# Two layers on one core: activation table sets loaded by name, a pair's output kept one step later, and the last four head pairs in a new order with rotary products on 32-row quarters

## The chip, the cores and the metric

One Trainium2 chip, one of its cores. The metric is the device time of one execution in microseconds (us), lower is better. Engine names: PE is TensorE, DVE is VectorE, ACT is ScalarE, POOL is GpSimd, SP is SyncE. The kernel is one hand-scheduled program: each engine runs its own list of instructions in order, and the lists meet only at semaphores.

## The reference, cut to what matters

512 tokens of width 1024 go through two different layers. The first is a feed-forward half, an attention part and another feed-forward half; the second is a modulated layer with a convolution, a chunked recurrence (rwkv) and a feed-forward part with a short convolution. The change touches the attention of the first layer and the activation functions of ACT.

```python
def chunked_relbias_attention(q, k, v, rel_bias):      # heads "A": 8 heads of 64, bias from a table
    ...
        sc = jnp.einsum('bihd,bjhd->bhij', q_blk, kb).astype(jnp.float32) * scale
        sc = sc + bias[None]
...
def mla_attention(c_q, c_kv, k_rope, ...):             # heads "B": 8 heads of 64 + 32
    q_nope = rmsnorm(q[..., :B_NOPE], q_nope_norm)
    q_pe = apply_rope(rmsnorm(q[..., B_NOPE:], q_rope_norm), cos, sin)
    k_nope = rmsnorm(kv[..., :B_NOPE], k_nope_norm)
    k_pe = apply_rope(rmsnorm(k_rope, k_rope_norm)[:, :, None, :], cos, sin)
    q_full = jnp.concatenate([q_nope, q_pe], axis=-1)
    k_full = jnp.concatenate([k_nope, jnp.broadcast_to(k_pe, (b, s, B_HEADS, B_ROPE))], axis=-1)
    return block_causal_attention(q_full, k_full, v)
```

So a score of a B head is a product over 64 "nope" rows plus a product over 32 rotary rows, and the rotary key is the same for all eight heads. In the second layer `sigmoid`, `tanh`, `exp`, `log`-based inverse roots and `silu` follow each other on ACT.

## The kernel before, in words

Activations lie with features on the 128 partitions and 512 tokens along the free axis. Weights come in 264 slabs of 128 x 1024 through a ring of four (`RING`); SP loads a slab, POOL splits it in a high and a low part (`split`, L607 and L609), and PE multiplies in three passes (`product`, L735 to L737).

**Attention.** Heads go in pairs `p` = 0 to 7 (0 to 3 are A heads, 4 to 7 are B heads), each with four blocks of 128 queries `qb` = 0 to 3 and `L` = 128 (qb + 1) keys. A step `t` is one pair and one block, in the order p, qb: 32 steps. PE runs a loop over `i`; in one turn of it stand, in this order, `scores(i + 1)`, `turn(i - 2)` (the transposes of the probabilities, L1032) and `values(i - 3)` (probabilities times values, L1048). Scores of A heads use 64 rows of the array for each of the two heads (L1018); those of B heads need 96 rows, so one head of a pair after the other (L1021), and SP first copies rows together for them (`rows_moved`, 24 transfers of its queue, L558 to L564). Beside PE:

- DVE at step `i`: `score_max(i)` (add bias or mask, row minimum, two instructions, L2185), `keep_turned(i - 3)` (PSUM to SBUF for the second head, L2200), `row_recip(i - 1)` (L2192), and where a pair ends `out_lo(p)` (L2205).
- ACT at step `i`: `keep_turned(i - 3)` for the first head (L1694), `softmax(i)` (two Exp, L1684), and where a pair ends `out_hi(p)` (L1699).
- POOL: `probs_scaled(t)` (L625), and in three of four steps of pairs 1 to 3 a part of the rotary embedding (L635 to L640).

The scores of a step lie in two of the banks 0 to 3, so `scores(t)` waits until DVE has read step t - 2 (`row_nmax`, 2 (t - 1)). The output of a pair lies in bank 6 + p % 2; the first `values` of pair p therefore waits for `out_lo(p - 2)`:

```python
if qb == 0 and p >= 2:
    pe.wait_ge(S("o_made"), p - 1)
```

`out_hi(p)` and `out_lo(p)` stand at `i == last_step(p) + 4`. At the end of the loop three products of the next stage (`out1_begun`) are put between the last steps of attention.

**Activation functions.** ACT holds one set of function tables at a time. Where a function is needed that is not surely loaded, the compiler puts a load before it (ACT_TABLE_LOAD in the trace). In the second layer `inverse_root` (L1758 Ln, L1761 Exp) runs in `key_rs` and `centred_rs`; `recurrence(half)` calls `key_rs(1)` in half 0 and `centred_rs(0)` in half 1, between moves of PSUM results (`move`, L1751) that PE waits for. `centred(1)` moves and squares the last results (L1751, L1853), and PE sums the squares (L1297) before it begins the product `out2`.

## Time and profile before

| | us |
|---|---|
| median of 3 runs | 1695.97 (1695.22 to 1697.27) |
| profiled execution, its own time | 1695.5 |
| span in the profile | 1693.7 |
| PE busy | 1652.9 |
| POOL, DVE, ACT busy | 998.2, 946.2, 429.6 |
| mean granted TensorE clock | 0.992 |

The profile shows one execution. The span runs from the first to the last recorded instruction; the execution's own time is 1.8 us longer. In timelines a row gives start, duration, engine, line, operation, output and inputs, shapes and how many records are merged; a matmul of plain float32 leaves two records. A bracket gives the idle time before the row and what ended it.

### The profile page before, as it was taken

Reading aid. Unit: us, or ns where it says so; the run is one execution under the profiler, and the core shown is the slowest. Engines: PE = TensorE matmul, PEld = TensorE weight load, DVE = VectorE, ACT = ScalarE, POOL = GpSimd, SP = SyncE. Lnnn points to the kernel's source line nnn. Section 1 sums busy time; section 2 is a strip of 40 time slices with the busy share of each in tenths; the row PEclk is TensorE's granted clock in tenths of the full one; section 3 lists DMA queues with packets and bytes.
Section 4 is the critical chain, followed back from the end, with each engine's and each line's share of the span. In section 5 each row is a group of like instructions: output and inputs, shape, how many; then the busy total and the mean of one; then the engine's idle time right before and its main releaser. Section 6 shows DMA issues by size and latency. Waiting matters only on the chain.

```text
span 1693.7 us, 26731 instructions
## 1 busy us (share of the span) xinstructions
PE 1652.9 (98%) x10086; PEld 1349.5 (80%) x10086; DVE 946.2 (56%) x1381; ACT 429.6 (25%) x713; POOL 998.2 (59%) x626
## 2 busy tenths in 40 slices
PE   8999999999999999999999999998989999999998
PEld 6888888888766778888888867887868788888887
DVE  5665551226656347555562259987766765665003
ACT  4000000015866321111100031234453333233001
POOL 3666666776565367666677744611205576666674
PEclk9999999999999999999999999999999899999999
DMA  6444443333241134444443322210002232233332
GB/s 211 145 149 148 142 144 124 100 99 125 77 118 45 51 110 144 141 149 149 149 149 104 107 90 73 92 63 3 3 2 91 72 99 94 92 99 99 102 110 87
DMA packets 52400, 175.80 MB, mean 104 GB/s; under 512 B 6369, under 2 KB 8801, under 8 KB 52193
## 3 DMA queue, kind: packets, MB, share of 16 engines
q1 hardware_dynamic: 43056, 144.64, 26.4%
q10 hardware_dynamic: 9264, 30.02, 5.6%
q8 instruction: 60, 0.98, 0.2%
q14 instruction: 20, 0.16, 0.0%
HBM read 169.66 MB, written 2.10 MB: 101 GB/s over the span
## 4 chain that ended last, share of the span: by engine, by line
PE 92%; DVE 3%; ACT 3%; issue 1%; POOL 1%; DMA 0%; ACTq 0%; DVEq 0%; POOLq 0%; SPq 0%
PE banks L735 25%; PE banks L736 25%; PE banks L737 25%; PE banks L1190 4%; PE banks L1021 1%; PE banks L1048 1%; PE banks L767 1%; PE banks L773 1%; PE banks L768 1%; PE banks L1032 1%; PE banks L855 1%; PE banks L1018 1%; PE banks L808 1%; PE banks L1165 1%; PE banks L810 0%
## 5 line engine op out<-in xcount | busy, mean ns | idle before, releaser
L609 POOL TENSOR_TENSOR w_lo<-w_raw,w_hi 128x1024 fp32r<-128x1024 f32 x256 | 635.2, 2481 | 21.4
L607 POOL TENSOR_SCALAR w_hi<-w_raw 128x1024 fp32r<-128x1024 f32 x256 | 288.9, 1129 | 546.5 <-DMA w_raw<-in_slabs 469.3
L735 PE MATMUL banks<-h_hi,w_hi 128*128 128x512 f32 x1376 | 539.8, 392 | 0.6 <-POOL w_lo L609 0.5
L737 PE MATMUL banks<-h_hi,w_lo 128*128 128x512 f32 x1376 | 535.6, 389 | 0.0
L736 PE MATMUL banks<-h_lo,w_hi 128*128 128x512 f32 x1376 | 535.4, 389 | 0.0
L735 PEld LDWEIGHTS banks<-h_hi,w_hi 128*128 128x128 f32 x1376 | 258.3, 188 | 61.4 <-issue 6.8
L736 PEld LDWEIGHTS banks<-h_lo,w_hi 128*128 128x128 f32 x1376 | 258.4, 188 | 54.0 <-issue 1.2
L737 PEld LDWEIGHTS banks<-h_hi,w_lo 128*128 128x128 f32 x1376 | 258.3, 188 | 53.7
L735 PE MATMUL banks<-act_hi,w_hi 128*128 128x512 f32 (+1 forms) x550 | 209.6, 381 | 0.0
L736 PE MATMUL banks<-act_lo,w_hi 128*128 128x512 f32 (+1 forms) x550 | 209.3, 381 | 0.0
L737 PE MATMUL banks<-act_hi,w_lo 128*128 128x512 f32 (+1 forms) x550 | 209.3, 381 | 0.0
L1630 ACT ACTIVATE tmp<-tmp 128x512 f32<-128x512 f32 x44 | 27.9, 634 | 360.9 <-DVE tmp L2033 360.9
L737 PEld LDWEIGHTS banks<-act_hi,w_lo 128*128 128x128 f32 x550 | 103.4, 188 | 19.9
L735 PEld LDWEIGHTS banks<-act_hi,w_hi 128*128 128x128 f32 x550 | 103.4, 188 | 19.9
L736 PEld LDWEIGHTS banks<-act_lo,w_hi 128*128 128x128 f32 x550 | 103.4, 188 | 19.4
L2073 DVE SCALAR_TENSOR_TENSOR xT<-banks,xT 128x512 f32<-128x512 f32 x24 | 16.6, 691 | 168.7 <-PE banks L737 168.7
L2033 DVE TENSOR_TENSOR tmp<-banks,tmp 128x512 f32<-128x512 f32 x44 | 30.5, 692 | 142.0 <-PE banks L737 137.8
L2025 DVE TENSOR_TENSOR act_lo<-tmp,act_hi 128x512 f32 x66 | 105.2, 1594 | 8.1
L2047 DVE CUSTOM_DVE_ANT_0 adaw<-adaw,silc 128x1024 f32<-128x1024 f32 x48 | 76.0, 1583 | 4.9 <-DMA adaw<-in_ada 4.5
L2589 DVE SCALAR_TENSOR_TENSOR tmp<-banks,vec,tmp 128x511 f32<-128x511 f32 x44 | 32.8, 746 | 75.8 <-ACT tmp L1925 75.8
L2038 DVE TENSOR_TENSOR tmp<-tmp 128x512 f32<-128x512 f32 x44 | 63.1, 1435 | 8.6 <-ACT tmp L1630 8.6
L1190 PEld LDWEIGHTS banks<-in_arena 64*64 64x64 f32 x1792 | 59.5, 134 | 10.5 <-issue 6.9
(384 smaller groups left out, 1837.6 us busy)
## 6 DMA issues: line engine op xcount, KB each, us to landing
w_raw<-in_slabs SPq DMA_DIRECT2D x260, 512.0 KB, 3.5
adaw<-in_ada ACTq DMA_DIRECT2D x48, 512.0 KB, 3.6
relb<-in_relb ACTq DMA_DIRECT2D x8, 256.0 KB, 2.9
out_y<-xT SPq DMA_DIRECT2D x16, 128.0 KB, 1.8
w_raw<-in_slabs SPq DMA_DIRECT2D x4, 256.0 KB, 5.3
xT<-in_x SPq DMA_DIRECT2D x1, 1024.0 KB, 8.9
block<-in_block ACTq DMA_DIRECT2D x1, 704.0 KB, 7.1
xT<-in_x SPq DMA_DIRECT2D x2, 256.0 KB, 3.9
```

Source lines behind the costliest of these rows:

```text
L607: nc.gpsimd.tensor_scalar(w_hi[:, r, :], w_raw[:, r, :], 1.0, 1.0, ALU.mult, ALU.mult).then_inc(S("w_hi"), 1)
L609: nc.gpsimd.tensor_tensor(w_lo[:, r, :], w_raw[:, r, :], w_hi[:, r, :], ALU.subtract).then_inc(S("w_split"), 1)
L735: mm(out, hi, rhs_hi, start=start, stop=False, skip_group_check=True)
L736: mm(out, hi, rhs_lo, start=False, stop=False, skip_group_check=True)
L737: return mm(out, lo, rhs_hi, start=False, stop=stop, skip_group_check=True)
L1190: last = mm(out, block_of(lhs, operands, e, g, c), r, start=opens and i == 0, stop=i == len(pairs) - 1, skip_group_check=True)
L1630: f(tmp[:, 2 + u, :], tmp[:, 2 + u, :], ACT.Silu).then_inc(S("silu"), 1)
L2025: v.tensor_tensor(actl_t[:, bass.ds(at * T, T)], t, hi, ALU.subtract).then_inc(S("act_lo"), 1)
L2033: v.tensor_tensor(tmp[:, 2 + u, :], bank[2 * u], tmp[:, 0, :], ALU.mult).then_inc(S("gate_scaled"), 1)
L2038: v.tensor_tensor(tmp[:, 4 + u, :], tmp[:, 2 + u, :], tmp[:, 4 + u, :], ALU.mult)\
L2047: v.tensor_tensor_reduce(out=adaw[:, u, :], in0=adaw[:, u, :], in1=silc, scale=1.0, scalar=0.0, op0=ALU.mult, op1=ALU.add, accum_out=mod_s ...
L2589: v.scalar_tensor_tensor(out=tmp[:, n, 1:T], in0=bank[n][:, 0:T - 1], scalar=w[1], in1=tmp[:, n, 1:T], op0=ALU.mult, op1=ALU.add).then_inc ...
```

## The change

Five places name a table set ahead of its use. Attention of the pairs 4 and 5, then 6 and 7, goes block by block with the two pairs in turn (4, 5, 4, 5, ...), and PE issues the scores of two steps together: four products on 64 rows, then four rotary products on 32 rows each that add to the same banks. The rotary key is copied to all four row quarters (three transfers) and the 24 transfers of `rows_moved` go. Probabilities of these steps use six slots instead of four (four tiles of the bias table are reused). `out_hi` and `out_lo` of pairs 0 to 5 stand at `last_step(p) + 5`. `turn(2)` stands ahead of `scores(5)`, and the third `out1_begun` behind the last `values`.

```diff
         def pair_step(t):
-            p, qb = divmod(t, NT)
+            if t < 4 * NT:
+                p, qb = divmod(t, NT)
+            else:
+                two, r = divmod(t - 4 * NT, 2 * NT)
+                p, qb = 4 + 2 * two + r % 2, r // 2
             return p, qb, P * (qb + 1)
...
         def prob_of(t, e):
-            return prob[:, 2 * (t % 4) + e, 0:pair_step(t)[2]]
+            n = 2 * (t % 4 if t < 4 * NT else (t - 4 * NT) % 6) + e
+            return (prob[:, n, :] if n < 8 else relb[:, n - 8, :])[:, 0:pair_step(t)[2]]
 
         def last_step(p):
-            return NT * p + NT - 1
+            return NT * p + NT - 1 if p < 4 else 4 * NT + 2 * NT * (p // 2 - 1) - 2 + p % 2
+
+        def kept_at(p):
+            return last_step(p) + (5 if p < 6 else 4)
...
-            def rows_moved():
...
+            def key_rows_copied():
+                sp.wait_ge(S("roped"), 3)
+                for a in range(32, P, 32):
+                    sp.dma_start(kr[a:a + 32, 0, :], kr[0:32, 0, :]).then_inc(S("key_rows"), 16)
...
             def scores(t):
...
-                if t >= 4 * NT and qb == 0:
-                    pe.wait_ge(S("rows_moved"), 96 * (p - 3))
                 if t >= 2:
                     pe.wait_ge(S("row_nmax"), 2 * (t - 1))
...
+                q, k = (qa, ka) if p < 4 else (qn, kn)
                 for e in range(2):
-                    mm(out[e][:, 0:L], head_rows(qn, p - 4, e)[:, qs], head_rows(kn, p - 4, e)[:, 0:L], start=True, stop=True)\
-                        .then_inc(S("scores"), 1)
+                    e64 = slice(CH * e, CH * e + CH)
+                    last = mm(score_bank(t, e)[:, 0:L], q[e64, p % 4, qs], k[e64, p % 4, 0:L], start=True, stop=p < 4,
+                              skip_group_check=True)
+                    if p < 4:
+                        last.then_inc(S("scores"), 1)
+
+            def rotary_scores(t):
+                p, qb, L = pair_step(t)
+                if t == 4 * NT:
+                    pe.wait_ge(S("key_rows"), 48)
+                pe.wait_ge(S("roped"), 6 if p < 6 else 9)
+                for i in range(4):
+                    r = slice(32 * i, 32 * i + 32)
+                    mm(score_bank(t + i // 2, i % 2)[:, 0:L], qr[r, (p - 4) // 2, P * qb:P * qb + P], kr[r, 0, 0:L],
+                       start=False, stop=True, skip_group_check=True).then_inc(S("scores"), 1)
...
             for i in range(8 * NT + 3):
                 if i == 2:
                     turn(1)
-                if 3 <= i + 1 < 8 * NT:
+                if i == 4:
+                    turn(i - 2)
+                if 3 <= i + 1 < 4 * NT:
                     scores(i + 1)
+                elif 4 * NT <= i + 1 < 8 * NT and (i + 1) % 2 == 0:
+                    scores(i + 1)
+                    scores(i + 2)
+                    rotary_scores(i + 1)
...
-                if 4 <= i < 8 * NT + 2:
+                if 5 <= i < 8 * NT + 2:
                     turn(i - 2)
                 if i >= 4:
                     values(i - 3)
-                if 8 * NT - 1 <= i < 8 * NT + 2:
-                    out1_begun(i - (8 * NT - 1))
+                if i >= 8 * NT - 1 and i != 8 * NT + 1:
+                    out1_begun((8 * NT - 1, 8 * NT, 8 * NT + 2).index(i))
...
                 for p in range(8):
-                    if i == last_step(p) + 4:
+                    if i == kept_at(p):
                         out_hi(p)
...
+            act.preload_act_table_set("silu_and_others")
             gate_up("gu2", KF)
...
             norm_hi("mixpre")
+            act.preload_act_table_set("sigmoid_and_others")
...
                     f(conv_rs, conv_rs, ACT.Exp, scale=-0.5).then_inc(S("second_std"), 1)
+                    act.preload_act_table_set("silu_and_others")
...
+                if m == 8:
+                    act.preload_act_table_set("natural_log_exp_and_others")
                 if m == 9:
                     key_rs(0)
...
             recurrence(1)
+            act.preload_act_table_set("natural_log_exp_and_others")
             centred(1)
             centred_rs(1)
...
-                    if t >= 4:
+                    if 4 <= t < 5 * NT:
                         dve.wait_ge(S(f"turned{e}"), t - 3)
+                    elif t >= 5 * NT + 2:
+                        dve.wait_ge(S(f"turned{e}"), t - 5)
...
                 for p in range(8):
-                    if i == last_step(p) + 4:
+                    if i == kept_at(p):
                         out_lo(p)
```

## Rows read from the trace of the kernel before

**Rows 1.** The page, part 1: busy time of each engine.
```profile
PE 1652.9 (98%) x10086; PEld 1349.5 (80%) x10086; DVE 946.2 (56%) x1381; ACT 429.6 (25%) x713; POOL 998.2 (59%) x626
```

**Rows 2.** Waits of the whole span: us in total, times, longest.
```profile
ACT tmp L1630 <- DVE tmp L2033: 360.9, 43, 10.3
...
PE banks L1032 <- DVE probT_odd L2200: 1.4, 3, 0.6
...
PE banks L1018 <- DVE small L2185: 0.6, 1, 0.6
```

**Rows 3.** Timeline of A heads, 506 to 516 us: one pair.
```profile
506.00 0.92 PE L1018 MATMUL banks<-ka,qa 64*128 64x384 f32 x4
...
508.68 1.13 PE L1018 MATMUL banks<-ka,qa 64*128 64x512 f32 x4
...
509.74 0.44 PE L1032 MATMUL banks<-both,prob 128*128 128x128 f32 x2
...
511.13 0.49 PE L1018 MATMUL banks<-ka,qa 64*128 64x128 f32 x4
...
511.55 0.66 PE L1032 MATMUL banks<-both,prob 128*128 128x128 f32 x4
...
512.66 0.69 DVE L2205 TENSOR_TENSOR h_lo<-banks,h_hi 128x512 fp32r<-128x512 f32 x1 [1.25 <-ACT h_hi L1699]
...
513.14 0.55 PE L1032 MATMUL banks<-both,prob 128*128 128x128 f32 x3
...
514.26 0.52 PE L1032 MATMUL banks<-both,prob 128*128 128x128 f32 x3 [0.57 <-DVE probT_odd L2200]
...
514.70 0.66 PE L1048 MATMUL banks<-probT_odd,va 128*64 128x128 f32 x8
...
515.29 0.92 PE L1018 MATMUL banks<-ka,qa 64*128 64x384 f32 x4
```

**Rows 4.** Timeline of B heads, 531 to 545 us: one pair.
```profile
531.47 0.58 ACT L1699 ACTIVATE h_hi<-banks 128x512 fp32r<-128x512 f32 x1
...
533.33 0.86 PE L1032 MATMUL banks<-both,prob 128*128 128x128 f32 x6
...
534.13 0.66 PE L1048 MATMUL banks<-probT_odd,vb 128*64 128x128 f32 x8
...
534.71 0.91 PE L1021 MATMUL banks<-kn,qn 96*128 96x384 f32 x2
...
535.66 0.56 DVE L2185 CUSTOM_DVE_ANT_0 prob<-banks,maskb 128x384 f32<-128x384 f32 x1 [0.80 <-PE banks L1021]
...
537.24 0.61 ACT L1684 ACTIVATE prob<-prob,small 128x384 f32<-128x384 f32 x1
...
544.85 0.91 PE L1021 MATMUL banks<-kn,qn 96*128 96x384 f32 x2
```

**Rows 5.** Timeline of PE in the second layer: products on 32 rows.
```profile
1035.59 1.13 PE L1258 MATMUL banks<-tmp,g2b 32*128 32x512 f32 x4
```

**Rows 6.** Timeline of recurrence(0) around key_rs(1).
```profile
1155.99 1.28 ACT L1758 ACT_TABLE_LOAD   x1
...
1157.29 1.07 ACT L1758 ACTIVATE banks<-banks 128x512 f32<-128x512 f32 x2
...
1160.29 0.69 DVE L2301 TENSOR_TENSOR silc<-silc,banks 128x512 f32<-128x512 f32 x1 [0.94 <-ACT banks L1761]
...
1161.84 0.68 PE L1190 MATMUL banks<-in_arena 64*64 64x64 f32 x16 [1.27 <-ACT in_arena L1751]
```

**Rows 7.** Timeline of PE in recurrence(1), behind centred_rs(0).
```profile
1228.04 0.68 PE L1190 MATMUL banks<-in_arena 64*64 64x64 f32 x16 [1.27 <-ACT in_arena L1751]
```

**Rows 8.** Timeline behind recurrence(1): centred(1) on ACT and PE.
```profile
1260.19 1.07 ACT L1751 ACTIVATE in_arena<-banks 128x512 f32<-128x512 f32 x2
...
1263.30 1.13 PE L1297 MATMUL banks<-tmp,block 128*128 128x512 f32 x2 [0.20 <-ACT tmp L1853]
```

**Rows 9.** Timeline of PE before the first low-rank product.
```profile
1006.93 1.13 PE L1249 MATMUL banks<-in_arena 64*128 64x512 f32 x4 [0.39 <-issue]
```

More of the change, by code:

```diff
@@ L487, in prob_of @@
         def prob_of(t, e):
-            return prob[:, 2 * (t % 4) + e, 0:pair_step(t)[2]]
+            n = 2 * (t % 4 if t < 4 * NT else (t - 4 * NT) % 6) + e
+            return (prob[:, n, :] if n < 8 else relb[:, n - 8, :])[:, 0:pair_step(t)[2]]
         def last_step(p):
-            return NT * p + NT - 1
+            return NT * p + NT - 1 if p < 4 else 4 * NT + 2 * NT * (p // 2 - 1) - 2 + p % 2
+        def kept_at(p):
+            return last_step(p) + (5 if p < 6 else 4)
         def score_bank(t, e):
             return bank[4 + 2 * t + e if t < 2 else 2 * (t % 2) + e]
-        def head_rows(m, p, e):
-            tile = (m, (qa, ka)[m is kn])[e]
-            return tile[0:96, p, :]
         rotary = [(kr[0:32, 0, :], tmp[0:32, 2, :]), (qr[:, 0, :], tmp[:, 4, :]), (qr[:, 1, :], tmp[:, 5, :])]
@@ L549, in rows_swapped @@
                         sp.dma_start(tmp[b:b + 16, 4:6, :], qr[c:c + 16, :, :]).then_inc(S("rope_in"), 16)
-            def rows_moved():
-                for p in range(4):
-                    sp.wait_ge(S("scores"), 2 * NT * (p + 1))
-                    if p:
-                        sp.wait_ge(S("rows_moved"), 96 * p)
-                    for m in (qn, kn):
-                        sp.dma_start(head_rows(m, p, 1)[0:CH, :], m[CH:P, p, :]).then_inc(S("rows_moved"), 16)
-                    sp.wait_ge(S("roped"), 6 if p < 2 else 9)
-                    sp.wait_ge(S("rows_moved"), 96 * p + 32)
-                    for e in range(2):
-                        at = 32 * ((2 * p + e) % 4)
-                        sp.dma_start(head_rows(qn, p, e)[CH:96, :], qr[at:at + 32, p // 2, :]).then_inc(S("rows_moved"), 16)
-                        sp.dma_start(head_rows(kn, p, e)[CH:96, :], kr[0:32, 0, :]).then_inc(S("rows_moved"), 16)
+            def key_rows_copied():
+                sp.wait_ge(S("roped"), 3)
+                for a in range(32, P, 32):
+                    sp.dma_start(kr[a:a + 32, 0, :], kr[0:32, 0, :]).then_inc(S("key_rows"), 16)
             for n in range(in1 * RING, (out1 + 1) * RING):
@@ L569, in _ @@
                 if n == SLAB_AT["out1"] + RING:
-                    rows_moved()
+                    key_rows_copied()
                 sp.wait_ge(S("slab_done"), n + 1 - RING)
@@ L1002, in scores @@
                 p, qb, L = pair_step(t)
-                out = [score_bank(t, e) for e in range(2)]
                 qs = slice(P * qb, P * qb + P)
@@ L1010, in scores @@
                     pe.wait_ge(S("in1_raw"), len(MADE) + 4)
-                if t >= 4 * NT and qb == 0:
-                    pe.wait_ge(S("rows_moved"), 96 * (p - 3))
                 if t >= 2:
                     pe.wait_ge(S("row_nmax"), 2 * (t - 1))
-                if p < 4:
-                    for e in range(2):
-                        e64 = slice(CH * e, CH * e + CH)
-                        mm(out[e][:, 0:L], qa[e64, p, qs], ka[e64, p, 0:L], start=True, stop=True).then_inc(S("scores"), 1)
-                    return
-                for e in range(2):
-                    mm(out[e][:, 0:L], head_rows(qn, p - 4, e)[:, qs], head_rows(kn, p - 4, e)[:, 0:L], start=True, stop=True)\
-                        .then_inc(S("scores"), 1)
+                q, k = (qa, ka) if p < 4 else (qn, kn)
+                for e in range(2):
+                    e64 = slice(CH * e, CH * e + CH)
[12 more added lines that the diff above has]
+                       start=False, stop=True, skip_group_check=True).then_inc(S("scores"), 1)
             def turn(t):
```

## The prediction

> **What bounds the kernel now.** I read the page first: PE is busy 1652.9 of 1693.7 us [rows 1], so only two things can move the time, work taken off PE and the 41 us in which PE waits. Next the list of waits, for PE's waits that the edited lines can reach: 1.4 us at the transposes L1032, 0.6 us at the scores L1018 [rows 2], and, hidden in general groups, two waits of 1.27 us behind ACT's moves [rows 6, 7]. Then the timelines of one pair of A heads and one of B heads. What the reader is to see: an A pair takes 9.29 us (506.00 to 515.29) and has a hole in it; a B pair takes 10.14 us (534.71 to 544.85) and has none [rows 3, 4]. B heads are bound by PE itself, A heads by PE and one wait.
>
> **The hole in an A pair.** The transposes of L = 384 start at 513.14 and the values behind them at 514.70: 1.56 us [rows 3]. Without a wait the same piece takes 0.80 us (533.33 to 534.13) [rows 4]. So the hole is 0.76 us. Its cause is two rows up: DVE stood 1.25 us at `out_lo` until ACT had made h_hi, and `keep_turned`, for which PE's second half of the transposes waits, stands behind it [rows 3]. One step later ACT has short Exps and DVE short reductions, so `out_lo` is met with slack. There are three such waits, 1.4 us in all, the longest 0.6 [rows 2], so two are like this one and the third is 0.4 us shorter: I take 0.76 + 0.76 + 0.36 = 1.9 us back. `turn(2)` ahead of `scores(5)` fills the single wait of 0.6 us [rows 2], of which I take 0.5. A heads: -2.4 us; from 0 (the wait only moves) to -2.5.
>
> **Scores of B heads on PE.** Work of a pair beside scores: an A pair free of its hole takes 9.29 - 0.76 = 8.53 us. Its scores take 0.42 us for L = 128 (511.13 to 511.55) and 1.06 for 512 (508.68 to 509.74) [rows 3]: 0.213 us for each 128 keys and 0.21 us fixed. Four blocks have 10 times 128 keys: 2.13 + 0.84 = 2.97 us. The rest is 5.56 us, so B scores take 10.14 - 5.56 = 4.58 us a pair, 18.3 in all. In the new form, two steps are two 64-row rounds and one 32-row round. That 32-row products run side by side is seen for two of them: their four records last 1.13 us, and so do those of two products on 64 rows [rows 3, 5]. With four abreast two pairs cost 3 x 2.13 = 6.4 us, and fixed parts. Each round that leaves its row form costs 0.21; I charge it twice in each of the 8 double steps, once between 64 and 32 rows and once behind: 2 x 6.4 + 16 x 0.21 = 16.2 us. Gain 2.1 us. Ends: if the inner change is free, 3.8; if the quarters go only two abreast, 4.3 us more work and a loss of 2.2.
>
> The Trainium skill ("TensorEngine Tiling (Array Packing)", Key Properties) says that a change of the tiling mode drains TensorE; it speaks against this edit, which adds one change in each double step. With it the sum is the 16.2 us above, without it 14.5; the 0.21 us of [rows 3] is what a trace shows of it.
>
> **What the new order makes wait.** Pairs 4 and 5 now begin in adjacent steps 16 and 17, and 6 and 7 in 24 and 25. `values(17)`, at i = 20, needs `out_lo(3)`, and `kept_at(3)` is 20 too; `values(25)`, at i = 28, needs `out_lo(5)`, kept at 28. Before, three steps lay between. Count from the end of the rotary products issued one turn of the loop earlier (L = 384 both times). DVE and ACT: reduction 0.56 and its accumulator, about 0.64; two Exps, 0.60 apart, 1.2; h_hi 0.58; `out_lo` 0.69 [rows 3, 4]; four hand-overs, 0.2 together: 3.3 us. PE has in the meantime a transpose group of 128 keys, values of 128 keys and transposes of 256 keys. By the same slope these are 0.14 + 0.21 n, so 0.36, 0.36 and 0.58, 1.3 us. The hole is at most 2.0 us; 0.4 of it is already lost at the transposes before it (below), so 1.6 each, 3.2 us.
>
> Further, all four score tiles of two steps now come free at once. DVE then has two reductions ahead of `keep_turned`: for L = 384, 0.1 of hand-over + 2 x 0.5 + 0.3 for the copy (estimated from the reduction's 0.56 [rows 4] and the shorter length) = 1.4 us, against 1.0 us until PE reaches the second half of its transposes (0.36 + 0.36 + 0.3). That is 0.5 us with the hand-over at turns 18 and 26, 0.3 to 0.4 each at 20, 28 and 29, by the same count with longer rows. `scores(19)`, which now needs step 17 read while DVE stands at `out_lo(2)`, loses 0.5. Together 2.5 us; between 0 (if all hides) and 4. Behind each of these waits stand PE's next transposes, and nothing but PE waits for those.
>
> Attention: -2.4 - 2.1 + 3.2 + 2.5 = +1.2 us.
>
> **Transfers.** The 24 transfers that go and the 3 that come stand on SP behind the loads of slabs that are split after attention. The next slab load waits for a ring slot that PE frees after the loop, so nothing on SP is earlier or later. The copies start once the rotary key is made, in the steps of pair 1, so two pairs ahead of step 16. The shifted `out1_begun` leaves the last `values` behind one `keep_turned` of some 0.7 us with about as much cover: 0.0 to 0.2 us. All at nothing.
>
> **Table sets.** A load takes 1.28 us and the next Ln starts 0.01 after it [rows 6]. In `key_rs(1)` two loads go (2.6 us), and with them the moves that PE waited 1.27 us for [rows 6]. But the keys' chain on DVE can advance only by its own idle 0.94 [rows 6], and a later step of PE waits for that chain, so I take 0.95. In `centred_rs(0)` PE's 1.27 us goes whole [rows 7], with a little of the next short hole: 1.35. The Tanh/Sigmoid pair makes PE's wait of 0.39 us [rows 9] vanish: 0.4. Against that, the set named before `centred(1)` stands between the move of y and the move of d, which follow without a gap in one row at 1260.19; from there ACT is what PE waits for until 1263.30 [rows 8]. One load of 1.28 us now lies on that path; the loads it saves came behind it, in the shadow of the first sixteen three-pass products of out2. +1.3. The loop of gu2 loses 11 loads, but there ACT waits 360.9 us for DVE in 43 waits [rows 2], so 0; the set named at m == 8 likewise, in a stage of products where the list shows no wait of PE for ACT. Sum: -0.4 - 0.95 - 1.35 + 1.3 = -1.4 us; ends 0 and -2.7.
>
> The Trainium skill ("ScalarE: Activation LUTs", What ACT_TABLE_LOAD costs) puts a drain of about 1.38 us beside the load of 1.28. By it each removed or added load would weigh 2.66 us, the last term +2.7, and the sum of the sets about -0.1 if PE's waits cap the gains; the start of the Ln at 0.01 us behind the load speaks against it.
>
> **Sum.** +1.2 - 1.4 = -0.2 us on the profiled execution, 1695.5 to 1695.3. It ran 0.5 under the median, so against the median 1695.97 I say 1695.8.
>
> **Rivals.**
> *The o waits hide (0.2).* If ACT and DVE run ahead of PE by a step when pairs 3 and 5 are kept, the 3.2 us vanish and about half of the 2.5: -0.2 - 3.2 - 1.3 = -4.7, so 1691.3. For it: DVE has slack in a B pair, 0.80 us before one reduction [rows 4]. Against: the Exps wait for scores issued just before, and idle time earlier does not help them.
> *The quarters don't run four abreast (0.1).* Only two are seen together [rows 5]. Two abreast adds 4.3 us: +4.1, so 1700.1, slower. It decides once the four products need a second round; a rotary group twice as long as a 64-row group of the same L would show it.
> *The names do nothing (0.1).* If the compiler still puts a load before Ln and Exp each, the sets give 0: 1697.2.
> *Forecast (0.6).*
>
> Less than 0.2%, 3.4 us, is about what a measurement of this kernel cannot tell from no change. The likeliest case alone spans 1693 to 1698. The range takes in the first rival below and reaches to the edge of the second above: 1690.5 to 1699.5. Faster by over 0.2% (under 1692.6): the first rival, most of it, and a sliver of the forecast, 0.22. Slower (over 1699.4): most of the second rival and a clock that falls in the longer hole before out2, 0.12. Within: 0.66.
>
> **What would show it.** Right: no wait at L1032 for probT_odd in A pairs, periods near 8.5 us; pairs 4 and 5 together near 22 us (11.1 + 8.1 + 1.6 + 1.25; 20.3 before); two PE waits of about 1.6 us at L1048 behind h_lo, at the first values of pairs 5 and 7; no loads at L1758 and L1761; the first out2 product 1.3 us further behind the d products. Wrong: no wait at those `values`, 32-row groups longer than 64-row ones, or Ln and Exp still with loads.

## The result and the profile after

The changed kernel takes 1698.15 us (median of 22 runs, 1693.86 to 1702.04) against 1696.03 for the kernel before on the same chip (22 runs, 1694.27 to 1697.32). The ratio is 1.0014, with a 95% interval of 1.0008 to 1.002: slower, by 2.1 us. The forecast was 1695.8 and no change. The time lies inside the range, but the sign is wrong: 2.1 us is less than the 3.4 us that I called the limit of a measurement, yet the interval, from 22 runs each, lies wholly above 1.

The profiled execution took 1698.04 us, its span is 1696.2 (before 1693.7). The page, span and busy time of each engine:

```profile
span 1696.2 us, 26805 instructions
...
PE 1654.3 (98%) x10150; PEld 1348.2 (79%) x10150; DVE 945.5 (56%) x1381; ACT 405.4 (24%) x694; POOL 1001.5 (59%) x626
```

ACT is 24 us less busy than before [rows 1]: 19 of its 74 table loads are gone. PE is 1.4 us busier, though it got score products that take less time. That is the first sign of something that the forecast does not have.

I set the same products of PE beside each other in both traces and took the difference of their starts, after minus before. Both start attention within 0.4 us of each other.

| stretch, by its first and last product | before | after | change |
|---|---|---|---|
| first scores to the scores of L = 384 of pair 3 | 483.37 to 515.29 | 482.98 to 512.77 | -2.13 |
| from there to the first product of ffn2 | to 611.73 | to 613.64 | +4.43 |
| to the first product after the next norm | to 982.08 | to 984.73 | +0.74 |
| to the first low-rank product [rows 9] | to 1006.93 | to 1008.94 | -0.64 |
| to the products behind key_rs(1) [rows 6] | to 1161.84 | to 1162.99 | -0.86 |
| to the first products behind them that wait for the keys | to 1224.86 | to 1227.13 | +1.12 |
| to the products behind centred_rs(0) [rows 7] | to 1228.04 | to 1229.32 | -0.99 |
| to the first product of y in centred(1) | to 1259.30 | to 1260.77 | +0.19 |
| to the first product of out2 | to 1263.86 | to 1266.55 | +1.22 |
| to the last transposes | to 1687.51 | to 1690.04 | -0.16 |

The sum is +2.92; less the 0.39 by which attention begins earlier it is the 2.53 between the spans. Attention is +2.30, where +1.2 was forecast. The sets gain 0.64 + 0.86 + 0.99 and lose 1.22, close to the forecast's 0.4 + 0.95 + 1.35 and 1.3. Three lines are in no part of the forecast: +0.74, +1.12 and the small +0.19.

The list of PE's waits after, from 500 to 565 us, and below it one row of the list for the whole span:

```profile
PE banks L1050 <- DVE h_lo L2221: 2.8, 2, 1.4
PE banks L1034 <- DVE probT_odd L2216: 0.9, 4, 0.3
PE banks L1010 <- DVE small L2201: 0.2, 1, 0.2
PE banks L1034 <- DVE probT_even L2216: 0.2, 1, 0.2
```

```profile
PE banks L1305 <- ACT tmp L1864: 1.4, 1, 1.4
```

The wait of 1.4 us at the transposes of A heads [rows 2] is gone, and two waits of 1.4 us at the values (L1050) stand in its place, both behind `out_lo` (L2221). The timeline of PE shows where:

```profile
526.78 1.56 PE L1010 MATMUL banks<-kn,qn 64*128 64x384 f32 x8
528.27 0.93 PE L1023 MATMUL banks<-kr,qr 32*128 32x384 f32 x8
529.12 0.44 PE L1034 MATMUL banks<-both,prob 128*128 128x128 f32 x2
...
530.61 0.41 PE L1034 MATMUL banks<-both,prob 128*128 128x128 f32 x2 [0.28 <-DVE probT_odd L2216]
532.43 0.44 PE L1050 MATMUL banks<-probT_odd,vb 128*64 128x128 f32 x4 [1.42 <-DVE h_lo L2221]
532.80 1.99 PE L1010 MATMUL banks<-kn,qn 64*128 64x512 f32 x8
534.72 1.14 PE L1023 MATMUL banks<-kr,qr 32*128 32x512 f32 x8
535.79 0.66 PE L1034 MATMUL banks<-both,prob 128*128 128x128 f32 x4
...
554.04 0.44 PE L1050 MATMUL banks<-probT_odd,vb 128*64 128x128 f32 x4 [1.42 <-DVE h_lo L2221]
554.41 3.23 PE L1010 MATMUL banks<-kn,qn 64*128 64x512 f32 x8
557.57 1.54 PE L1023 MATMUL banks<-kr,qr 32*128 32x512 f32 x8
559.04 0.66 PE L1034 MATMUL banks<-both,relb 128*128 128x128 f32 x4
```

Three things are to be read here. First, four products on 32 rows of L = 512 last 1.14 us as a group, as two products on 64 rows do (1.13) [rows 3]: the quarters run four abreast. Second, the two waits stand where they were named, at 1.42 us each. Third, the same products take 2.99 us behind the first wait (532.80 to 535.79) and 4.63 us behind the second (554.41 to 559.04). The table by stretches (core 0; the number behind POOL's is PE's granted clock) says why:

```profile
552.00:554.00 2.00, 0.41 (x2) 0.20 (x2) 0.84 (x4) 1.53 (x6) 0.93 (x2) 1.00 0.00 0
554.00:556.00 2.00, 1.96 (x10) 1.08 (x12) 1.34 (x6) 1.31 (x4) 0.56 (x2) 0.75 0.01 4
556.00:558.00 2.00, 2.00 (x8) 0.50 (x10) 0.00 (x0) 0.00 (x0) 0.58 (x2) 0.50 0.00 0
558.00:560.00 2.00, 2.00 (x18) 0.88 (x16) 0.87 (x3) 0.46 (x2) 0.00 (x0) 0.89 0.00 0
```

PE stood from 552 to 554 for most of the time (busy 0.41 of 2.00), and then its clock fell from 2.4 to 1.2 GHz. The price is 4.63 - 2.99 = 1.64 us, more than the wait itself.

At the other end of the kernel, ACT and PE around centred(1):

```profile
1261.64 0.58 ACT L1761 ACTIVATE in_arena<-banks 128x512 f32<-128x512 f32 x1
1262.24 1.28 ACT L1904 ACT_TABLE_LOAD   x1
1263.53 0.60 ACT L1761 ACTIVATE in_arena<-banks 128x512 f32<-128x512 f32 x1
```

```profile
1264.84 2.27 PE L1305 MATMUL banks<-tmp,block 128*128 128x512 f32 x4 [1.45 <-ACT tmp L1864]
```

The named set stands between the two moves, as read off [rows 8], and PE's wait for the d products has grown from 0.20 to 1.45 us. In the recurrence Ln and Exp follow their move without a load (compare [rows 6]):

```profile
1157.53 0.60 ACT L1761 ACTIVATE in_arena<-banks 128x512 f32<-128x512 f32 x1 [1.27 <-PE banks L1198]
1158.02 1.08 ACT L1768 ACTIVATE banks<-banks 128x512 f32<-128x512 f32 x2
1159.01 1.07 ACT L1771 ACTIVATE banks<-banks 128x512 f32<-128x512 f32 x2
```

Last, the +1.12 us. In the recurrence, at lines that the change does not touch, PE stands twice within 4 us, and the profile names nothing that it waits for (it writes `issue`):

```profile
1181.29 0.21 PE L1225 MATMUL banks<-in_arena,in_h 64*64 64x64 f32 x1 [0.24 <-issue]
...
1184.96 0.27 PE L1427 MATMUL banks<-in_h,in_arena 64*64 64x64 f32 x1 [0.77 <-issue]
```

A third such gap, of 0.19 us, stands at L1225 at 1248.34 and is the +0.19 of the table. Before, none of the three is in the trace.

### The profile page after: what moved, and what is told of

Read it like the earlier page. It is cut to its first block, busy times and chain, and to the rows that moved or that the text cites. A ratio compares the mean times of both kernels' runs of the same rounds, so it can differ in the third digit from the quotient of the medians.

```text
span 1696.2 us, 26805 instructions
## 1 busy us (share of the span) xinstructions
PE 1654.3 (98%) x10150; PEld 1348.2 (79%) x10150; DVE 945.5 (56%) x1381; ACT 405.4 (24%) x694; POOL 1001.5 (59%) x626
## 4 chain that ended last, share of the span: by engine, by line
PE 93%; DVE 3%; ACT 2%; issue 1%; POOL 1%; DMA 0%; ACTq 0%; SPq 0%; DVEq 0%; POOLq 0%
PE banks L730 25%; PE banks L732 25%; PE banks L731 25%; PE banks L1198 4%; PE banks L1010 1%; PE banks L1050 1%; PE banks L762 1%; PE banks L768 1%; PE banks L763 1%; PE banks L1034 1%; PE banks L850 1%; PE banks L1173 1%; PE banks L803 1%; PE banks L805 0%; PE banks L804 0%
## 5 line engine op out<-in xcount | busy, mean ns | idle before, releaser
L2061 DVE CUSTOM_DVE_ANT_0 adaw<-adaw,silc 128x1024 f32<-128x1024 f32 x48 | 101.4, 2113 | 4.6 <-DMA adaw<-in_ada 4.3
L2039 DVE TENSOR_TENSOR act_lo<-tmp,act_hi 128x512 f32 x66 | 91.9, 1393 | 8.1
L1198 PE MATMUL banks<-in_arena 64*64 64x64 f32 (+1 forms) x1792 | 62.4, 231 | 3.6 <-issue 3.3
```

The costliest lines, as they stand in the source:

```text
L1198: last = mm(out, block_of(lhs, operands, e, g, c), r, start=opens and i == 0, stop=i == len(pairs) - 1, skip_group_check=True)
L2039: v.tensor_tensor(actl_t[:, bass.ds(at * T, T)], t, hi, ALU.subtract).then_inc(S("act_lo"), 1)
L2061: v.tensor_tensor_reduce(out=adaw[:, u, :], in0=adaw[:, u, :], in1=silc, scale=1.0, scalar=0.0, op0=ALU.mult, op1=ALU.add, accum_out=mod_s ...
```

## The experiments

Each time is the median of 5 to 11 runs, set against the kernel before on the same chip; its median was 1696.0, 1696.56, 1695.93 and 1695.7 us in the four batches. Where kernels of different batches are compared, I compare their ratios. An interval is about 1.5 us wide to either side, and 2.0 to 2.3 with 5 or 6 runs, so of differences near 1 us the trace decides, not the time. A trace shows one execution; I count it from its first scores to its last transposes where executions reached attention at different times.

### Do the two waits cost what they seem to, and is the clock theirs?

**e3_kept_early**: o kept one step later for pairs 0 to 2 alone.

```diff
-            return last_step(p) + (5 if p < 6 else 4)
+            return last_step(p) + (5 if p < 3 else 4)
```

> The changed kernel, with the outputs of pairs 3 to 5 kept at last_step + 4 again (pairs 0 to 2 stay at + 5). Theory W (the two waits of values(17) and values(25) for out_lo, 1.42 us each, and the half clock of 1.6 us behind the second are what the new order lost): both waits go, the clock stays at 1.00 around 554 us, and the kernel is 4 to 4.5 us faster than the changed one: about 1694, ratio to before 0.9988. Rival F (the fixed cost of two row forms and DVE's full queue eat the gain, the o waits only show it): new waits of the same size come up at the transposes, and the time stays within 1 us of the changed kernel, 1697 to 1699.

Measured: 1695.81 us, ratio 0.9996 (0.9987 to 1.0005), 3.0 us under the changed kernel. No wait for h_lo is left, and the clock is 1.00 from 552 to 560. The waits are real. By the medians the gain is 1 to 1.5 us less than I expected; by the traces attention, up to the first product of ffn2, is 4.30 us shorter (126.36 against 130.66).

**e7_kept5**: the same edit with `p < 5`, so that pair 3 keeps its wait and only pair 5 loses it.

> The changed kernel with pair 5's o kept one step earlier (pairs 0 to 4 as in the change). My theory: the profile after shows two waits of 1.42 us at the values, behind h_lo of pairs 3 and 5, and behind the second the granted clock falls to half and a double step's score products take 1.6 us longer. Then the first wait of 1.42 us must stay, the second be gone, and with it the fall of the clock: 1.4 + 1.6 = 3.0 us faster than the changed kernel, about 1695.2, the same as before within 0.1%. Rival: the fall of the clock has nothing to do with the wait (it would come at this place anyway): 1.4 us faster only, 1696.7, and the score products of 64x512 at half clock are still there. Second rival: both waits move to the transposes behind: no gain, 1698.1.

Measured: 1696.95 us, ratio 1.0003 (0.9994 to 1.0013), 1.9 us under the changed kernel; its span is 4.0 us shorter. Of that 3.1 us lie in attention, where 3.0 was expected, and 0.8 in the norm before the mix, where the half clock lasts less long. PE, and the stretches where the clock had fallen:

```profile
532.54 0.44 PE L1050 MATMUL banks<-probT_odd,vb 128*64 128x128 f32 x4 [1.42 <-DVE h_lo L2221]
...
552.65 0.44 PE L1050 MATMUL banks<-probT_odd,vb 128*64 128x128 f32 x4
553.02 1.99 PE L1010 MATMUL banks<-kn,qn 64*128 64x512 f32 x8
554.93 1.14 PE L1023 MATMUL banks<-kr,qr 32*128 32x512 f32 x8
```

```profile
554.00:556.00 2.00, 2.00 (x14) 0.49 (x10) 0.00 (x0) 0.34 (x2) 0.82 (x2) 1.00 0.03 8
556.00:558.00 2.00, 1.84 (x20) 1.29 (x17) 1.91 (x7) 1.50 (x4) 0.09 (x1) 1.00 0.00 0
```

The first wait stays, the second is gone, and with it the fall of the clock: the products are back at 1.99 and 1.14 us. The rival, a fall that would come at this place anyway, is out. It is not the second wait as such, though. Three more kernels keep both waits. In two of them (e2, e15) the clock falls behind the second, in e8_attention behind the first, and there alone:

```profile
531.13 0.44 PE L1050 MATMUL banks<-probT_odd,vb 128*64 128x128 f32 x4 [1.42 <-DVE h_lo L2215]
531.50 3.05 PE L1010 MATMUL banks<-kn,qn 64*128 64x512 f32 x8
534.48 1.72 PE L1023 MATMUL banks<-kr,qr 32*128 32x512 f32 x8
```

So each of the four profiled executions with both waits has one fall, behind the one or the other. None of the others has any fall in attention. With one wait left (e7) the profile has none. It is a profile of the fastest of e7's executions (1693.95 us; they go up to 1699.62), and the time has won 1.9 us where the trace has 4.0, which suggests that some executions do fall there. That is an inference, no trace shows it.

**e5_hi_first**: h_hi ahead of the Exps in ACT's step, everything else as in the change.

```diff
+                for p in range(8):
+                    if i == kept_at(p):
+                        out_hi(p)
                 if i < 8 * NT:
                     softmax(i)
...
-                for p in range(8):
-                    if i == kept_at(p):
-                        out_hi(p)
```

> The changed kernel with h_hi put ahead of the two Exps in ACT's loop step, all kept steps as in the change. My theory: the wait at values(17) and values(25) is a chain reduction, two Exps, h_hi, out_lo; without the two Exps it is 1.2 us shorter each time, so of 1.42 us some 0.2 is left, and the clock does not fall: 2.4 + 1.6 = 4.0 us off, less 1 to 1.5 us for the Exps that now stand behind h_hi: 2.5 to 3 faster than the changed kernel, 1695.1 to 1695.6. Rival: ACT's order does not matter because DVE is the late engine (its reductions stand ahead of out_lo): within 0.5 us of the changed kernel and both waits still above 1 us.

Measured: 1694.34 us, ratio 0.999 (0.9981 to 0.9999), 4.0 us under the changed kernel. Each wait for h_lo shrinks from 1.42 to 0.16 us:

```profile
551.37 0.44 PE L1050 MATMUL banks<-probT_odd,vb 128*64 128x128 f32 x4 [0.16 <-DVE h_lo L2221]
551.74 1.99 PE L1010 MATMUL banks<-kn,qn 64*128 64x512 f32 x8
```

So the chain is the one that the prediction counted (reduction, two Exps, h_hi, `out_lo`), with the Exps its largest link. The gain is above what I expected: putting the Exps behind h_hi cost nothing that the list of waits shows.

### What is each part worth alone?

**e1_sets**: the kernel before with the five named sets and nothing else. **e8_attention**: the changed kernel without them. **e4_o_later**: the kernel before, its scores and order as they were, with `turn(2)` ahead of `scores(5)` and `kept_at` of the change.

> The kernel before with the five named sets and nothing else. Theory as in the prediction: PE's two waits of 1.27 us behind ACT's moves go, 1.3 us come in before the sums of squares (L1297): 1.4 us faster than before, ratio 0.9992. If only what the trace of the changed kernel shows is real (about 1.0 in recurrence(0), 1.0 in recurrence(1), 1.2 lost), 0.8 us faster, ratio 0.9995. Rival: with the drain of the clock's level after the longer wait the loss is 2 us or more and the ratio 1.000 or above.

Measured: 1693.59 us, ratio 0.9984 (0.9975 to 0.9993). The sets are worth 2.4 us by the medians; the profiled execution's span is 1.5 us shorter.

> The changed kernel without the five named sets: attention alone. If the sets bring 2.0 us in the recurrences and cost 1.3 behind them (net -0.7 to -1.4 us), this is 0.7 to 1.4 us slower than the changed kernel: 1699 to 1699.5, ratio to before 1.0018 to 1.0022. If the sets' loss at centred(1) outweighs what they give, this is faster than the changed kernel, 1697.

Measured: 1697.13 us, ratio 1.001 (1.0001 to 1.0019). A miss: without the sets the changed kernel is 0.7 us faster by the ratios (1.0 by the medians), where I expected it 0.7 to 1.4 slower. The intervals overlap. The profiled execution reached the first scores 1.3 us earlier, before any edit, and from there to the last transposes it takes 1208.81 us against 1207.06. In that count the sets are worth 1.75 us, but it is not theirs: 1.86 us of difference lie behind the first product of out2, past the last set, in a norm where e8's clock stays at half longer, and the two executions differ in other falls too. So neither number settles it; the waits of single lines do: 1.27 and 1.26 us behind the two moves here, 0.28 us with the sets.

> The kernel before with the outputs of pairs 0 to 5 kept one step later and turn(2) ahead of scores(5), in the old order of pairs and with scores on 96 rows. Theory W: the three waits for probT_odd and the one at scores(5) go and no wait for out_lo comes, since a pair begins four steps behind the one before: 2.1 to 2.4 us faster, ratio 0.9987. Rival: the later output delays the first values of the next pair but one also in this order, and the time stays that of before.

Measured: 1693.83 us, ratio 0.9985 (0.9976 to 0.9994). So this edit alone gives the gain forecast for the A heads' hole, 2.2 us by the medians and 2.72 in the trace's attention.

So two parts of the change, each put on the kernel before by itself, are over 2 us faster than it. What turns the sum is the third, the new form and order of the B heads: in the old order the later output makes no wait for `out_lo`, in the new one it makes two. With the gaps below, that is where both gains go.

### The set ahead of centred(1)

**e2_set_moved**: the changed kernel; **e11_early_moved**: the same edit on e3_kept_early.

```diff
-            act.preload_act_table_set("natural_log_exp_and_others")
             centred(1)
+            act.preload_act_table_set("natural_log_exp_and_others")
             centred_rs(1)
```

> The changed kernel with the last named set moved behind the moves of centred(1), ahead of its Ln. My theory: the load of 1.28 us no longer stands between the move of y and the move of d, PE's wait of 1.45 us at the first product of the d group goes down to the 0.2 us of before, and the load is hidden where the loads of Ln and Exp were: 1.2 us faster than the changed kernel, about 1696.9. Rival: the load, wherever it stands on ACT before out2, is paid, so no gain: 1698.1, with the same distance from the d products to the first product of out2 or a longer one.

Measured: 1697.86 us, ratio 1.0007 (0.9998 to 1.0016), 0.3 us or, by the ratios, 1.2 us under the changed kernel: the time can't tell. The trace can:

```profile
1262.84 2.27 PE L1305 MATMUL banks<-tmp,block 128*128 128x512 f32 x4 [0.23 <-ACT tmp L1864]
...
1264.55 0.79 PE L730 MATMUL banks<-h_hi,w_hi 128*128 128x512 f32 x1
```

The wait is 0.23 us, and from the first product of y to the first of out2 it takes 4.71 us against 5.78: 1.07 us back.

> The changed kernel with o kept early (pairs 0 to 2 alone one step later) and the last set behind centred(1). My theory: the wait of 1.45 us before the d products goes and nothing takes its place: 1.2 us faster than the same kernel with the set in front of centred(1), which stood 0.2 us under before: 1694.6 to 1695.0. Rival: the moved set gains nothing in the end (in the changed kernel alone it moved the time by 0.3 us and the span of the profile by 1.4): 1695.8, though the wait is gone.

Measured: 1692.5 us, ratio 0.9981 (0.9972 to 0.999), by the ratios 2.5 us under e3_kept_early where 1.2 was expected. The direction is right, and two things beside the set differ in the traces. Its gaps in the recurrence are 0.24, 0.50 and 0.18 us against 0.51 and 0.70 in e3_kept_early, 0.3 us less, and the granted clock from 1187 to 1190 us is 1.00 against 0.50.

### Everything mended, and the old order with the same edits

**e9_later_sets**: the kernel before with e4's edits and the sets, the last one behind centred(1). **e10_old_hi**: that with h_hi first. **e6_all**: the changed kernel with the edits of e3, e5 and e2.

> The kernel before with o kept one step later, turn(2) ahead, and all five sets, the last of them behind centred(1); scores and order of the B heads as before. My theory: the parts add up. o one step later alone measured 2.2 us faster than before and the five sets alone 2.4; moving the last set gives another 1.2: 5 to 6 us faster than before, about 1690.2 to 1691.2. Rival: what the sets gain is lost again in a clock that falls at another place, so that the sum is no more than the larger of the two, 2.4: 1693.6.

Measured: 1689.81 us, ratio 0.9963 (0.995 to 0.9977). It is 6.3 us faster than the kernel before, more than the 5 to 6 expected, and beats both kernels.

> The kernel with the old order and scores, o one step later and all five sets, the last one behind centred(1) (measured 1689.8), and now h_hi ahead of the Exps too. My theory: in this order the trace shows no wait of PE for h_lo, so h_hi ahead of the Exps finds nothing to shorten: within 0.5 us of 1689.8. Rival: the step order of ACT holds PE up in small waits everywhere: 1 us or more faster.

Measured: 1689.7 us, ratio 0.9965 (0.9951 to 0.9978). Nothing more, as the lack of a wait for h_lo in that order says.

> The changed kernel (score products on row quarters, new order) with all its waits mended: o kept one step later for pairs 0 to 2 alone, h_hi ahead of the Exps, the last set behind centred(1). My theory: without the two waits and the fall of the clock, PE's saving of 2.1 us on the scores must at last show. Against the kernel with o kept early alone (0.2 us faster than before) it gains about 0.8 us by h_hi ahead and 1.2 by the moved set: 2.2 to 3 us faster than before, 1693.5 to 1694.3. If the saving on PE were still whole it would stand at or below the old order with the same edits (1689.8). Rival: the new order's bursts (four score tiles freed at once) go on costing more than the 2.1 us that the quarters save, so that it stays 3 us or more above the old order: that is what tells them apart, 1689.8 or less against 1692.8 or more.

Measured: 1693.17 us, ratio 0.9982 (0.9973 to 0.9991), 3.2 us above the old order. By my own bounds this spoke for bursts that cost more than the quarters save. The traces say otherwise. Both kernels start the first low-rank product at the same moment, 1004.02 us, so attention with all that goes before is even: from the first scores to the first product of ffn2 it takes 125.70 us here and 125.64 in e9. What the quarters save, 2.1 us of score products, is used up inside attention, 1.05 us of it in five waits of PE for the turned probabilities that the old order does not have; no row names the rest. The 3 us arise between there and the first d product (1259.16 against 1256.10), in code that is the same in both. PE of e6_all:

```profile
1176.80 0.21 PE L1225 MATMUL banks<-in_arena,in_h 64*64 64x64 f32 x1 [0.79 <-issue]
...
1180.74 0.27 PE L1427 MATMUL banks<-in_h,in_arena 64*64 64x64 f32 x1 [1.25 <-issue]
```

I went through the recurrence of all thirteen kernels that had run. The eight with the new form of the B heads all have gaps of this kind, one at L1427 of 0.50 to 1.25 us, one before it at L1225 of 0.24 to 0.79, and seven of them a third at L1225 in the second half, 0.18 to 0.57. The five with the old form (before, e1, e4, e9, e10) have none.

### Where the gaps come from

The page lists a DMA queue that carries instructions, 61 packets and 1.00 MB in the changed kernel, so 16 KB each. In e6_all it brings three between 1172 and 1184 us, close to the gaps (packets, MB, share):

```profile
q8 instruction: 3, 0.05, 2.2%
```

The traces tie these packets to the gaps more closely than that. There are 26 gaps of this kind in the nine kernels that have them (the eight, and e13 below), and each ends 1.20 to 1.58 us after a packet of 16 KB has landed. And the packets go with PE: from 1160.4 to 1217.1 us of the changed kernel's trace ten more of them start, while PE starts 2516 instructions, about 252 for each. That they are PE's code, and that PE stands for want of it, is my reading; the profile names no such wait.

The new form of the B heads puts 32 more products of PE ahead of the recurrence, which are 128 more instructions, less 3 waits: 125. The traces have 11095 instructions of PE ahead of the same product of the recurrence before, and 11220 after. The Trainium skill ("Perfetto Trace Analysis", The 4-stage abstract model) says that an instruction has 64 bytes. By that, as an estimate, 125 of them are half a packet and 256 a whole one, which the 252 of the trace bear out. The gaps would then depend on where a packet ends in the dense run of short products. I tried it: waits that are always met, put between the long products of `project`, the first projections of the second layer, where they add instructions and nothing else.

```diff
+            spare = [0]
+            def spare_wait():
+                if spare[0] > 0:
+                    spare[0] -= 1
+                    pe.wait_ge(S("o_made"), 8)
+                    pe.wait_ge(S("x_new"), 8)
...
                 mm(out, hi, rhs_hi, start=start, stop=False, skip_group_check=True)
+                spare_wait()
                 mm(out, hi, rhs_lo, start=False, stop=False, skip_group_check=True)
+                spare_wait()
...
+            spare[0] = 131
             at = SLAB_AT["in2"]
```

Each `spare_wait` adds one instruction to PE (the other wait rides on the product behind it). **e12_all_shifted** is e6_all with 131, **e15_changed_shifted** the changed kernel with 131, **e13_later_shifted** e9_later_sets with 125, **e14_later_turned** the same with 256.

> The changed kernel with all waits mended (measured 1693.2), and 131 waits that are always met added to PE among the long projections before the recurrence, so that PE's code behind them lies a whole 256 instructions behind that of the kernel before (the change itself puts 125 in). Theory (gaps named issue come from where the code lies in the 16 KB packets of the instruction queue): the gaps in the recurrence, 0.79 and 1.25 us at 1176.80 and 1180.74, go, and the time falls by 1.6 to 3 us, to 1690.2 to 1691.6. Rival (they belong to the new order in some other way, or to chance): the gaps stay and the time is 1693.2 or a little more.

Measured: 1690.94 us, ratio 0.997 (0.9958 to 0.9982), 2.0 to 2.2 us under e6_all. The intervals touch; the trace is plain: the gaps are gone, and from the recurrence's first product behind a gap of 0.98 us, which every kernel has, to the first of out2 it takes 122.77 us against 125.75.

> The kernel with the old order, o one step later and the sets (measured 1689.8), with 125 such waits added to PE: its code behind them now lies as in the changed kernel. Theory: gaps named issue appear at the same lines of the recurrence (0.5 us or more each at the second y products and behind them), and the time rises by 1.6 to 3 us, to 1691.4 to 1692.8, with nothing else changed. Rival: no gaps, 1689.8 within 0.5 us.

Measured: 1691.27 us, ratio 0.9971 (0.9961 to 0.998), 1.5 us above e9_later_sets by the medians and 1.4 by the ratios, whose intervals overlap. Again the trace decides, 124.68 us for the same stretch against 122.80. All three gaps are there, 0.24, 0.50 and 0.29 us, at the same lines as in the changed kernel (L1434 here is L1427 there):

```profile
1179.74 0.27 PE L1434 MATMUL banks<-in_h,in_arena 64*64 64x64 f32 x1 [0.50 <-issue]
```

> The same with 256 waits: the code lies as in the kernel with the old order again, only one packet later. Theory: no gaps, and 1689.8 within 0.5 us; this shows also that the waits as such cost nothing among the long products. Rival (waits as such cost, or any shift of the code does harm): 1691 or more.

Measured: 1689.68 us, ratio 0.9964 (0.995 to 0.9977). No gap and no loss (122.76 us for the stretch): the waits cost nothing, and neither does a shift by 256.

The group of this line in PE's list from 1172 to 1184 us, in e6_all, e12, e13 and e14, one fence each (busy, mean ns of one, then idle time before it):

```profile
L1427 PE MATMUL banks<-in_h,in_arena 64*64 64x64 f32 x64 | 2.7, 219 | 1.2 <-issue 1.2
```

```profile
L1436 PE MATMUL banks<-in_h,in_arena 64*64 64x64 f32 x64 | 2.5, 218 | 0.0
```

```profile
L1434 PE MATMUL banks<-in_h,in_arena 64*64 64x64 f32 x64 | 2.6, 219 | 0.5 <-issue 0.5
```

```profile
L1434 PE MATMUL banks<-in_h,in_arena 64*64 64x64 f32 x64 | 2.3, 218 | 0.0
```

The clock belongs to the price here too, if less surely. The stretch behind the gaps in e6_all, and the same in e12:

```profile
1184.00:1188.00 4.00, 3.44 (x58) 2.98 (x58) 3.33 (x10) 0.21 (x1) 0.00 (x0) 0.64 0.01 4
```

```profile
1184.00:1188.00 4.00, 3.40 (x81) 2.92 (x81) 3.23 (x10) 0.60 (x1) 1.44 (x1) 1.00 0.01 4
```

In e13 it is 0.66, in e14 1.00. But it is no law. Of the nine kernels with the gaps seven have the fall, e8_attention (gaps of 0.56 and 1.24 us) and e11 have none; of the eight without gaps three have it (before, with 0.65 from 1188 to 1192, e1 and e4). Against the kernel before, the changed one loses by the gaps here and not by the clock.

> The changed kernel itself with the 131 waits. Theory: its gap of 0.77 us at 1184.96 and the smaller one at 1181.29 go: 0.8 to 2.5 us faster than the changed kernel (1698.15), 1695.7 to 1697.3, the two waits for h_lo and the fall of the clock unchanged. Rival: 1698.2 with the gaps where they were.

Measured: 1697.97 us, ratio 1.0013 (1.0004 to 1.0022). The gaps are gone, and so is the fall behind them; from the first scores to the first product of out2 the trace is 2.29 us shorter than the changed kernel's (781.28 against 783.57). It loses 1.59 us of that behind it, where the clock from 1300 to 1330 is 0.77 against 0.83. e8_attention and e13 lose as much there, the fourteen other kernels don't, so I can't lay it on the edit. The time shows nothing of the gain, 0.2 us by either count: a miss.

## Why the prediction was wrong

The kinds of effect named in the prediction all came, at nearly the size given. The sum fell short by effects that it did not have.

**What held.** The hole of the A heads: 2.13 us in the changed trace and 2.2 alone by the medians, against 2.4. The scores of the B heads: the four double steps last 1.08, 1.70, 2.34 and 2.99 us, twice that is 16.22; the prediction said 16.2, with two changes of row form at 0.21 us each. That fits the drain at a change of form that the Trainium skill ("TensorEngine Tiling (Array Packing)", Key Properties) states. The trace puts it at 0.2 us each, but no run changes the form alone, so a fixed cost of another kind is not excluded. The o waits: two, at the first values of pairs 5 and 7, 1.42 us each against 1.6. The further waits: 1.3 us by the list against 2.5; with 0.75 us that no row names, the rest of the stretch comes to 2.05. The sets: -1.3 us between attention and the last transposes against -1.4, with each of the four items within 0.4 us of its forecast. The drain of about 1.38 us that the Trainium skill ("ScalarE: Activation LUTs", What ACT_TABLE_LOAD costs) puts beside a load is not seen: the move behind the load starts 0.01 us after it, and moving the load away gave back 1.07 us.

**The step that failed.** "Attention: -2.4 - 2.1 + 3.2 + 2.5 = +1.2 us." Each wait was priced at its own length. The second one also takes the clock, and the products behind it run at 1.2 GHz: +1.64 us. Without that wait the fall is gone (e7_kept5), without either there is none. In e8_attention the first wait takes the clock instead, and the products behind it last the same 4.63 us (531.50 to 536.13), so the cost belongs to the pair of waits and not to this one alone. The prediction knew such a fall only "in the longer hole before out2", as a part of the slower chance, and not in the hole that it had itself forecast; the kernel before has full clock all through attention. Attention measured +2.30: the forecast's +1.2, plus 1.64, less 0.36 and 0.45 by which the waits came out smaller, plus 0.27 for the A heads.

**The term that was missing.** "Sum. +1.2 - 1.4 = -0.2 us on the profiled execution" takes code that is not touched to run as before. 125 instructions more ahead of the recurrence open 1.20 us of gaps in it (0.24, 0.77 and 0.19). e12, e13 and e14 show that the number of instructions is the cause: 125 more bring the gaps, 256 more don't, in either form of the B heads. That it acts through the packets is shown by their landings alone. Nothing in the trace of before gives its size, but the page's instruction queue and the short products of the recurrence could have been named.

**Chance.** The norm before the mix (+0.74 us) ran with a longer stretch at half clock in the changed kernel's profile (granted clock 0.83 against 0.89 from 970 to 1000), and in eleven more of the seventeen kernels, five of them with the old form. That I can't lay on the change. What I forecast, with 1.64 and 1.20 added, is -0.2 + 2.84 = +2.64 us, beside 2.5 in the spans and 2.1 in the medians; the agreement is closer than the parts are known. That the time lay inside the range says little: the range was wide enough for a gain of 5.5 us and a loss of 3.5.

**The rivals.** "The o waits hide" and "The quarters don't run four abreast" are refuted by the two rows at 532.43 and 534.72; "The names do nothing" by the missing loads. What came was the forecast's mechanism and two costs that it had no price for.

**Still open.** Why the clock falls behind one wait of 1.42 us and not behind the other, as long. Why e3_kept_early gains 3.0 us by its runs, where its trace is 4.0 shorter from the first scores to the last transposes; e5_hi_first agrees with its own, 4.0 and 4.15. Where the 0.75 us in attention go. And whether the quarters can be made to pay. With all mended and the gaps gone (e12) the new form stands 1.2 us above the old one by ratios whose intervals overlap, and even with it in the traces: from the first scores to the last transposes 1199.10 us, against 1199.09 in e14 and 1198.82 in e9. So its products take 2.1 us less and nothing of that reaches the end.

## What to carry to other kernels

A wait forecast on PE is to be priced with the products behind it at both clock levels; here one wait of 1.42 us cost 3.06. A part that saves PE time is worth only what the order it needs leaves of it: try the cheap edits on the old order first; here the output one step later, `turn(2)` ahead and the named sets gave 6.3 us there. And when code that nobody touched gets slower, look for gaps named issue, and shift the code with waits that are always met before blaming the edit.

## What the runs showed of the hardware

- Four fp32 products on 32 rows of different quarters, 512 columns each, take 1.14 us together (0.93 for 384, 0.71 for 256, 0.50 for 128), within 0.01 us of two products on 64 rows where both are shown (1.13 for 512, 0.92 for 384, 0.49 for 128).
- A queue of kind `instruction` brings packets of 16 KB all through the run (61 in the changed kernel), one for each 252 instructions of PE in the recurrence. Where short products follow densely (64 columns), PE can stand 0.18 to 1.25 us without a named cause, dependent on 125 or 131 instructions more or less ahead of them; each of 26 such gaps ends 1.20 to 1.58 us after a packet has landed.
- The same wait of 1.42 us can leave the granted clock at 1.00 or be followed by 0.50. Of two such waits, 21.6 us apart or 23.3, exactly one had a fall behind it in each of four traces, three times the second and once the first (e8_attention).
- Loads for Ln and Exp in turn vanish when the set that holds both is named ahead. Naming five sets took away 19 loads and with them 24 us of ACT's busy time; 1.3 to 2.4 us of that reach the end.
